# Feed-forward of a two-layer decoder step: up half of each feature tile convolved, multiplied and split by thirds of the tokens

## The reference

```python
u = rmsnorm(x, lw['norm_ffn']) @ lw['ffn_w_up']                 # 1024 -> 2 * 2816
u_pad = jnp.concatenate([buf0.astype(u.dtype), u], axis=1)
wc = lw['ffn_conv']
uc = sum(u_pad[:, j:j + T] * wc[j] for j in range(CONV_W)) + lw['ffn_conv_b']   # CONV_W = 3
gate, up = jnp.split(uc, 2, axis=-1)
x = x + (jax.nn.silu(gate) * up) @ lw['ffn_w_down']
```

## Time and profile before

| What | Value |
|---|---|
| Median of 3 runs | 3598.74 us (3596.16 to 3599.44) |
| Profiled execution, its own time | 3601.51 us |
| Its span, first to last instruction | 3598.6 us |
| PE busy | 3118.9 us, 87% |
| DVE busy | 1586.1 us, 44% |
| ACT busy | 1065.8 us, 30% |
| POOL busy | 86.3 us, 2% |
| Mean granted TensorE clock | 0.92 of full speed |

### The profile page before, as it was taken

The page is one execution under the profiler, slowest core; times in us unless marked ns, Lnnn a source line. Parts: engine busy times, 40 slices in busy tenths (PEclk is TensorE's granted clock), DMA queues, the critical chain, the costliest instruction groups (busy, mean ns, idle before and its releaser), DMA issues. The chain is left out here.

```text
span 3598.6 us, 49024 instructions
## 1 busy us (share of the span) xinstructions
PE 3118.9 (87%) x19116; PEld 2871.3 (80%) x19116; DVE 1586.1 (44%) x2506; ACT 1065.8 (30%) x1963; POOL 86.3 (2%) x216
## 2 busy tenths in 40 slices
PE   4998689477999999997979967983979999999976
PEld 4987555277999999997979956551979999999876
DVE  5233435135445455547351333440365544544564
ACT  4221223123332333234142212331243233233331
POOL 0000000000000000000000000000000000000000
PEclk9998689789999999998989967996989999999998
DMA  5100220421111111102030011205111111111023
GB/s 197 46 24 32 76 98 2 147 107 51 48 48 48 48 48 48 38 25 85 37 115 36 21 59 53 88 24 171 59 66 48 45 48 47 48 47 36 17 89 127
DMA packets 58323, 224.70 MB, mean 62 GB/s; under 512 B 6634, under 2 KB 22506, under 8 KB 42994
## 3 DMA queue, kind: packets, MB, share of 16 engines
q1 hardware_dynamic: 58098, 221.46, 17.2%
HBM read 193.92 MB, written 27.52 MB: 62 GB/s over the span
## 5 line engine op out<-in xcount | busy, mean ns | idle before, releaser
L149 PE MATMUL psum<-h_parts_ffn,conv_ffn_weight_parts 128*128 128x352 f32 x2112 | 684.2, 324 | 38.7 <-DVE h_parts_ffn L233 30.8
L150 PE MATMUL psum<-h_parts_ffn,conv_ffn_weight_parts 128*128 128x352 f32 x2112 | 679.7, 322 | 0.0
L151 PE MATMUL psum<-h_parts_ffn,conv_ffn_weight_parts 128*128 128x352 f32 x2112 | 679.4, 322 | 0.0
L1760 DVE SCALAR_TENSOR_TENSOR conv_sum<-u_padded,vectors,conv_sum 128x1024 f32<-128x1024 f32 x176 | 226.1, 1285 | 578.3 <-ACT conv_sum L1710 565.8
L149 PEld LDWEIGHTS psum<-h_parts_ffn,conv_ffn_weight_parts 128*128 128x128 f32 x2112 | 398.0, 188 | 42.5 <-issue 38.1
L150 PEld LDWEIGHTS psum<-h_parts_ffn,conv_ffn_weight_parts 128*128 128x128 f32 x2112 | 398.5, 189 | 0.0
L151 PEld LDWEIGHTS psum<-h_parts_ffn,conv_ffn_weight_parts 128*128 128x128 f32 x2112 | 398.4, 189 | 0.0
L149 PE MATMUL psum<-g_parts,conv_ffn_weight_parts 128*128 128x352 f32 x1056 | 345.9, 328 | 27.3 <-DVE g_parts L1771 16.3
L151 PE MATMUL psum<-g_parts,conv_ffn_weight_parts 128*128 128x352 f32 x1056 | 343.8, 326 | 0.0
L150 PE MATMUL psum<-g_parts,conv_ffn_weight_parts 128*128 128x352 f32 x1056 | 343.6, 325 | 0.0
L1779 DVE TENSOR_TENSOR x<-x,psum 128x352 f32<-128x352 f32 x528 | 255.5, 517 | 120.1 <-PE psum L151 119.7
(11 more groups left out here) (308 smaller groups left out, 5500.3 us busy)
## 6 DMA issues: line engine op xcount, KB each, us to landing
conv_ffn_weight_stage<-w_up_dram SPq DMA_DIRECT2D x44, 1024.0 KB, 4.8
conv_ffn_weight_stage<-w_down_dram SPq DMA_DIRECT2D x22, 1024.0 KB, 4.8
_projection_weight_stage<-w_in_dram SPq DMA_DIRECT2D x18, 1024.0 KB, 4.8
pages<-cache_dram SPq DMA_DIRECT2D x48, 320.0 KB, 4.8
pages<-cache_dram SPq DMA_DIRECT2D x48, 192.0 KB, 3.0
mix_work<-x_residual SPq DMA_DIRECT2D x16, 528.0 KB, 4.3
x<-x_residual SPq DMA_DIRECT2D x2, 4224.0 KB, 16.5
x_residual<-x SPq DMA_DIRECT2D x16, 528.0 KB, 2.7
```

Source lines behind the costliest of these rows:

```text
L149: pe.matmul(out, lhs[0], rhs[0], start=first, stop=False)
L150: pe.matmul(out, lhs[0], rhs[1], start=False, stop=False)
L151: return pe.matmul(out, lhs[1], rhs[0], start=False, stop=last)
L1760: dve.scalar_tensor_tensor(t[:, q, 0:SEQ], row[:, tap:tap + SEQ], w, t[:, q, 0:SEQ], ALU.mult, ALU.add).then_inc(ph["conv_step"], 1)
```

## The change

The gate half goes as before. The up half goes third by third on DVE: for each third c, `conv` waits for that third's evacuation alone, adds the two taps on 352 columns (for the last third 320 of the prompt and 32 of the samples), waits for SiLU, and multiplies that third. `g_hi`, `g_lo` and the opening waits of the down job go by thirds too, with the semaphore counts to match (CONV_STEPS is 12). In the changed kernel the gate taps are L1761 and L1763, the taps by thirds L1775 and L1779, the product L1784, the high part L1721, the low part L1790, the addition to x L1799.

```diff
@@ ACT @@
                 if not first:
                     act.wait_ge(ph["tail_made"], f)
-                    act.wait_ge(ph["glo_made"], f)
+                    act.wait_ge(ph["glo_made"], f * NC)
...
-                act.wait_ge(ph["conv_step"], f * 8 + 4)
+                act.wait_ge(ph["conv_step"], f * CONV_STEPS + 4)
                 act.activation(t[:, 0, :], t[:, 0, :], ACT.Silu).then_inc(ph["silu_made"], 1)
 
             def g_hi(f, slot, down_done=None):
-                act.wait_ge(ph["g_made"], f + 1)
                 if down_done is not None:
                     act.wait_ge(ph["mm_done"], down_done)
-                act.activation(gp[:, 0, slot, :], t[:, 1, :], ACT.Copy).then_inc(ph["ghi_made"], 1)
+                for c in range(NC):
+                    act.wait_ge(ph["g_made"], f * NC + (c + 1))
+                    act.activation(gp[:, 0, slot, chunk(c)], t[:, 1, chunk(c)], ACT.Copy)\
+                       .then_inc(ph["ghi_made"], 1)
@@ DVE @@
+                row = u[:, 1]
+                for c in range(NC):
+                    dve.wait_ge(ph["u_free"], f * UP_G + (NC + c + 1))
+                    at, n = c * CH, CH if c < NC - 1 else SEQ - 2 * CH
+                    per_tap = 1 if c < NC - 1 else 2
                     for i, tap in enumerate((1, 0)):
-                        w = vec[:, ds1(tile * CONV_W + V_CW + tap)]
+                        w = vec[:, ds1((f + FT) * CONV_W + V_CW + tap)]
                         if i:
-                            dve.wait_ge(ph["conv_step"], base + 2)
...
+                            dve.wait_ge(ph["conv_step"], f * CONV_STEPS + (4 + 2 * c + per_tap))
+                        dve.scalar_tensor_tensor(t[:, 1, at:at + n], row[:, tap + at:tap + at + n], w,
+                                                 t[:, 1, at:at + n], ALU.mult, ALU.add)\
                            .then_inc(ph["conv_step"], 1)
-                dve.wait_ge(ph["silu_made"], f + 1)
-                dve.wait_ge(ph["conv_step"], f * 8 + 8)
-                dve.tensor_tensor(t[:, 1, :], t[:, 0, :], t[:, 1, :], ALU.mult).then_inc(ph["g_made"], 1)
+                        if c == NC - 1:
+                            dve.scalar_tensor_tensor(tokens(t[:, 1]), samples(row)[:, :, tap:tap + DEC_SEQ], w,
+                                                     tokens(t[:, 1]), ALU.mult, ALU.add)\
+                               .then_inc(ph["conv_step"], 1)
+                    dve.wait_ge(ph["silu_made"], f + 1)
+                    dve.wait_ge(ph["conv_step"], f * CONV_STEPS + (4 + 2 * c + 2 * per_tap))
+                    dve.tensor_tensor(t[:, 1, chunk(c)], t[:, 0, chunk(c)], t[:, 1, chunk(c)], ALU.mult)\
+                       .then_inc(ph["g_made"], 1)
 
             def g_lo(f, slot):
-                dve.wait_ge(ph["ghi_made"], f + 1)
-                dve.tensor_tensor(gp[:, 1, slot, :], t[:, 1, :], gp[:, 0, slot, :].bitcast(F32),
-                                  ALU.subtract).then_inc(ph["glo_made"], 1)
+                for c in range(NC):
+                    dve.wait_ge(ph["ghi_made"], f * NC + (c + 1))
+                    dve.tensor_tensor(gp[:, 1, slot, chunk(c)], t[:, 1, chunk(c)],
+                                      gp[:, 0, slot, chunk(c)].bitcast(F32),
+                                      ALU.subtract).then_inc(ph["glo_made"], 1)
@@ PE, down @@
                 pe.wait_ge(ph["lo_made"], j + 1)
-                pe.wait_ge(ph["glo_made"], i * 2 + 2)
                 for t_ in range(KX):
                     for c in range(NC):
                         n = t_ * NC + c
+                        if n < NC:
+                            pe.wait_ge(ph["glo_made"], i * (2 * NC) + (NC + c + 1))
```

More of the change, by code:

```diff
@@ L1610, in conv_ffn @@
     STEP_G = 2 * UP_G + DOWN_G
+    CONV_STEPS = 4 + 2 * NC + 2
     with ExitStack() as st:
@@ L1750, in conv @@
             def conv(f):
[L1752 to L1755, removed]
+                row = u[:, 0]
+                dve.wait_ge(ph["u_free"], f * UP_G + NC)
+                for i, tap in enumerate((1, 0)):
+                    w = vec[:, ds1(f * CONV_W + V_CW + tap)]
+                    if i:
+                        dve.wait_ge(ph["conv_step"], f * CONV_STEPS + 2)
+                    dve.scalar_tensor_tensor(t[:, 0, 0:SEQ], row[:, tap:tap + SEQ], w, t[:, 0, 0:SEQ],
+                                             ALU.mult, ALU.add).then_inc(ph["conv_step"], 1)
+                    dve.scalar_tensor_tensor(tokens(t[:, 0]), samples(row)[:, :, tap:tap + DEC_SEQ], w,
+                                             tokens(t[:, 0]), ALU.mult, ALU.add)\
+                       .then_inc(ph["conv_step"], 1)
@@ L1760, in conv @@
[L1760 to L1763, removed]
-                           .then_inc(ph["conv_step"], 1)
-                dve.wait_ge(ph["silu_made"], f + 1)
```

## The result

The changed kernel takes **3609.25 us** (median, 3608.12 to 3617.68, 7 runs); the kernel before, in 7 runs beside it, 3599.44 (3596.16 to 3602.38). The ratio is 1.0035 with a 95% interval of 1.0026 to 1.0045, so it is slower by 9 to 16 us. Forecast were 3610.4 and a range of 3605.0 to 3618.0.

A forecast was written before the change was run, and what follows sets the result against it. PE, busy 87% of the span, was taken as the bound, so only its waits count. +14.2 us in the loop and -2.5 at the last down jobs made +11.7 on 3598.7: 3610.4 us, range 3605.0 to 3618.0.

The forecast's parts named there:

- The wait for SiLU holds taps that are ready: On DVE in the loop, the last two thirds' taps stand behind the wait for SiLU; DVE idles 0.89 us.
- The release: From SiLU's end on ACT to the first product's start on DVE: taken as 0.10 us, between 0.03 and 0.17.
- Durations and spacing: On DVE: taps 581 ns on 352 columns, 547 on 320, product 518; next instruction 0.08 us early if independent, 0.04 late otherwise.
- The chain from the first product to the weight split: On DVE behind SiLU: 4.08 us start to start, putting the weight split 0.71 us later than before.
- PE's wait: At group 8 of the loop's down jobs, waiting for an addition: from 0.55 to 1.26 us, 20 times, +14.2 us.
- The prediction's other half: In the loop, an earlier end of DVE's up-half chain can give back at most 0.55 us per PE wait.
- The last down jobs: At each layer's last down job PE starts 1.24 us earlier, pause 6.9 in place of 8.16 us; -2.5 us for two.
- What was taken as free: Extra high parts on ACT, low parts on DVE, PE's extra waits and the longer chain before the loop cost no time.
- The sum: Whole kernel: +14.2 in the loop and -2.5 at the last down jobs, +11.7 us, giving 3610.4 on the median.
- the four rivals: Whole kernel: additions earlier, 3585.2 (3%); little lost, about 3604 (9%); clock falls, 3660 (3%); more lost, over 3616.2 (7%).
- The first, SiLU in time: In the loop, SiLU done before the second third's taps are due, so PE's wait vanishes: -11.0, 3585.2 us; chance 3%.

The follow-up runs named there:

- e_behind: The changed kernel with the wait for SiLU and the three products moved behind the taps of all thirds; 3577.53 us, ratio 0.9934 to before.
- e_silu: The changed kernel with SiLU moved on ACT to behind the evacuation of the up half's first third, DVE's code unchanged; 3575.11 us, ratio 0.9935 to before.
- the fastest kernel: The changed kernel with SiLU earlier on ACT and, for some tiles, g's high and low parts made between the thirds; 3564.97 us, ratio 0.9905 to before.

## Why the prediction was right, step by step

**The wait for SiLU holds taps that are ready.** Right, and shown twice: the wait alone costs 19 to 31 us in the kernel before, and taking it from ahead of the taps, or meeting it early, turns the loss into a gain. The release that I put at 0.10 us between two rows was 0.12 (3362.59 to 3362.71); DVE's idle 0.89 was 0.92.

**Durations and spacing.** A tap by thirds and a product of the changed kernel (ns min/median/max), against the earlier trace rows:

```profile
L1775 DVE SCALAR_TENSOR_TENSOR conv_sum<-u_padded,vectors,conv_sum x264: 544/580/586, 895.3 to 3413.3; 128x352 f32<-128x352 f32 x88, 128x320 f32<-128x320 f32 x44
```

```profile
L1784 DVE TENSOR_TENSOR conv_sum<-conv_sum x132: 524/525/529, 897.6 to 3414.1; 128x352 f32<-128x352 f32 x132
```

A tap on 352 columns was forecast at 581 ns and is 580 to 586, on 320 at 547 and is 544 and up; the product takes 525, not 518. The chain from the first product to the weight split was forecast at 4.08 us and is 4.06. The pointer's 0.11 us is not paid between the two taps of the second and of the last third, as the order of instructions had shown. By the rule that the Trainium skill gives in "VectorE: DVE Perf Modes", "The DRAIN you can't avoid", the chain would have been 4.30, and the measured 4.06 decides against it here: three products in a row span 1.39 us where three durations of 0.525 are 1.58. The prediction left out that the same section has an operation that isn't held start earlier; with that the early start of the independent ones agrees.

**PE's wait.** Forecast 1.26 us, 20 times, +14.2; measured 1.27 and 25.4 - 11.0 = +14.4. The loops grew by 7.7 and 6.9 us, +14.5; in the second trace of the same kernel, with the same waits, by 7.4 and 5.8, +13.3. The prediction's other half, that an earlier chain can give back 0.55 us a stop at most, was too low: e_behind and e_silu gave back 0.83.

**The last down jobs.** Forecast 6.92 us and -2.5 in all; measured 6.91 and 16.3 - 13.8 = -2.5.

**What was taken as free.** It was: the first down job comes at the same time after the first matmul, and no new wait is among PE's. The granted clock stayed at 1.00 in both loops, through stops of 1.27 us.

**The sum.** Forecast +11.7; the two traces of the changed kernel show +11.0 and +9.1 in the stage, the medians 9.8 and 12.2. What the sum lacked is, in the main, the last down job itself, which ran up to 1.3 us shorter or 0.5 longer with the stretch at half clock behind the pause; in the second trace the loops are also 0.9 below the forecast's +14.2, which no wait shows. The last down job differs by as much between layers and traces of one kernel, so that the median came within 1.2 us of the forecast is in part luck. The wait, the chain and the pause, each forecast by itself, are not.

None of the four rivals (22% together) came. The first, SiLU in time, was priced at 3585.2; made true by the edit on ACT it is 3575.11. That price left the pause at the ends at 6.92 us, where it became 3.73, and missed 0.28 us for each stop (see the next section but one).

## What to carry to other kernels

Cutting an operation into pieces lets each start early only if nothing ahead of it in its engine's queue waits for something later; look up where the producer of that wait stands in its own queue, and place the wait behind all work that is ready, or move the producer. A piece costs its fixed part again: here 0.78 us a tile for cutting the taps and the product of one half into thirds, so what the early pieces take off the path has to exceed that. And find the consumer that pays: PE didn't wait for g in the loop at all, it waited for additions that were queued behind g.

## What the runs showed of the hardware that I had not expected

**A stop of PE costs more than its idle row says.** The waits of 0.55 us were 11.0 us in all; taking them away shortened the two loops by 16.6 us (e_behind) and 16.5 (e_silu), 0.83 us a stop. PE's rows of before around show where it goes:

```profile
3350.72 0.32 PE L150 MATMUL psum<-g_parts,conv_ffn_weight_parts 128*128 128x352 f32 x1
3350.88 0.32 PE L151 MATMUL psum<-g_parts,conv_ffn_weight_parts 128*128 128x352 f32 x1
...
3352.02 0.32 PE L150 MATMUL psum<-g_parts,conv_ffn_weight_parts 128*128 128x352 f32 x1
```

Matmuls start every 0.16 us, but the row's idle time is counted from the modelled end, 0.32 behind the last start; so 0.72 us are lost ahead of the matmul, and it takes 0.26 to the next one in place of 0.16, another 0.10. With a longer stop the surplus stays what it is: PE's waits grew by 0.72 us and the loops by 0.69 to 0.77 a stop in the first trace of the changed kernel.

**The clock can fall after a pause of 2.36 us.** In the fastest kernel both last down jobs wait 2.36 us; in layer 0 the granted clock went to half (1.2 GHz) behind it, in layer 1 it didn't. The windows of layer 0 and PE's rows (the wait, then the last matmul started at full pace before the fall and the first at half pace), and the windows of layer 1:

```profile
1618.00:1620.00 2.00, 0.00 (x0) 0.00 (x0) 1.40 (x5) 0.50 (x1) 0.21 (x1) 1.00 0.39 149
1620.00:1622.00 2.00, 1.99 (x8) 1.99 (x9) 1.05 (x3) 0.93 (x2) 0.00 (x0) 0.63 0.14 54
```

```profile
1620.02 0.43 PE L149 MATMUL psum<-g_parts,conv_ffn_weight_parts 128*128 128x352 f32 x1 [2.36 <-DVE g_parts L1762]
1620.28 0.32 PE L150 MATMUL psum<-g_parts,conv_ffn_weight_parts 128*128 128x352 f32 x1
...
1620.65 0.49 PE L149 MATMUL psum<-g_parts,conv_ffn_weight_parts 128*128 128x352 f32 x1
```

```profile
3376.00:3378.00 2.00, 1.95 (x12) 1.95 (x13) 1.38 (x3) 1.04 (x3) 0.00 (x0) 1.00 0.16 60
```

The clock fell some 0.5 us after PE had resumed and came back by 1624.08, which goes with 1.5 us more for that down job (27.24 against 25.73). After the pauses of 6.8 to 9.2 us the stretch at half clock varies too, and the down job with it (24.5 to 26.0 us); after 3.7 and 4.5 us it was there in both layers (24.7 all four times). The Trainium skill, "TensorE: Matmul & The Clock Gate", Part 1: The HAM clock gate, has the gate driven by the activity it sees, on a schedule of its own that a kernel doesn't set, and with that the difference between the two layers agrees. Why this pause was enough is not settled.

**GpSimd's copy took longer while DVE ran a tap.** The copies of 16 columns by POOL (ns min/median/max), before and after:

```profile
L1677 POOL COPY conv_tail<-u_padded x88: 192/698/1267, 891.7 to 3393.2; 128x16 f32 x80, 128x16 f32<-128x16 f32 x8
```

```profile
L1678 POOL COPY conv_tail<-u_padded x88: 193/196/564, 895.3 to 3409.9; 128x16 f32 x80, 128x16 f32<-128x16 f32 x8
```

Before, the first of a tile's two started 0.11 us behind the start of a tap of 1.28 us (3344.84) and took 1.23 us; now DVE is idle then, and it takes 0.20. POOL's busy time fell from 86.3 to 40.7 us. Nothing waited for it, so the time didn't change by it; the Trainium skill's page "SBUF — State Buffer", section "SBUF: two separate sides", has DVE operations with two SBUF inputs and GpSimd share a pair of ports that one holds for a whole instruction, and the rows agree.
